# Two transformer blocks on one core: four of the eight norms taken apart, with the rows' roots applied behind the products

## The chip, the core and the metric

One core of a Trainium2 chip runs the whole program: TensorE (PE in the profile, with its weight loads as PEld), VectorE (DVE), ScalarE (ACT), GpSimd (POOL) and SyncE (SP), which issues most of the transfers. The metric is the device time of one execution in microseconds (us), a median over several executions. Lower is better.

## The reference

Input x is 512 tokens of 1024 features. Block one is an attention block (forgetting attention and sparse attention, their outputs gated by two sigmoids) and a mixture of experts. Block two is a feed-forward network (FFN1), a mixer (neighbourhood attention and latent attention) and a second feed-forward network (FFN2). Cut to the norms that the change touches:

```
rms_norm(x, g) = x * rsqrt(mean(x*x) + 1e-6) * g

h = rms_norm(x, norm_mix_g)                        # norm 0, then h @ w_in, 4896 columns
...q, k, v of both attentions; g_a, g_b = last 2048 columns of h @ w_in
x = x + (sigmoid(g_a)*out_a + sigmoid(g_b)*out_b) @ w_out
x = x + moe(rms_norm(x, norm_ffn_g))               # norm 1, stays as it is
f = swiglu(rms_norm(x, ffn1_pre_g), w_gu, w_down)  # norm 2:  (silu(gate) * up) @ w_down
h = x + 0.5 * rms_norm(f, ffn1_post_g)             # a norm behind a stage ("post norm")
z = rms_norm(h, mix_pre_g) @ w_in_2                # norm 3
h = h + rms_norm(mixed, mix_post_g)                # post norm
f = swiglu(rms_norm(h, ffn2_pre_g), ...)           # norm 4
h = h + 0.5 * rms_norm(f, ffn2_post_g)             # post norm, the output
```

## The kernel before

Tokens are four tiles `t` of 128 rows. `xres` (in `xarea`) holds the residual rows, `hn` (in `harea`) the normed rows, `hT_hi` and `hT_lo` (in `tarea`) the features turned, features on the partitions and the 512 tokens along the row. All large products are made three times in fp32r, high by high, high by low, low by high (`products`, L420 to L422): a float is its rounded high part plus what is left. Weights come in units of 128x2048 (1 MB, `feed`, two buffers `raw`); ACT makes the high part of a unit (`split_high`, L405) and DVE the low part (`split_low`, L411). A unit takes 48 products of 128x512 on PE.

At a norm the engines work one after another: ACT squares four tiles and sums them (`norm_squares`, L1486), DVE scales the sum, ACT takes the root, DVE the reciprocal (`row_rstd`), DVE multiplies the rows by the root and the gain (`norm_rows`, L1775), PE turns them in 32 small transposes (`to_features`, L1015), ACT copies the high part out of PSUM (`to_hT`, L1494) and DVE makes the low part (`low_features`, L1803). The first unit's products are taken in parts (`products_in_parts`, L432, L433, L438), so that those that don't need the low features come first. A post norm is `post_squares` (L1501) and `post_norm` (L1790 and L1792: two instructions for each tile). Each engine is a queue in program order; semaphores tie them, and no scheduler moves anything.

Such a turn stands at five places: at the start (norm 0), behind the attentions (norm 1, for the experts), before FFN1 (norm 2), between FFN1 and the mixer (a post norm and norm 3) and between the mixer and FFN2 (a post norm and norm 4). The program ends with a post norm. In an FFN half (`ffn_half`) PE makes gate and up of a chunk `v` (11 chunks a half) in two banks, ACT applies Silu to the gate (L1659), DVE multiplies by up (L2149), ACT and DVE split the result (L1663, L2154), and the down products follow, whose banks 0 to 3 wait for the last chunk (`ff_hid`).

In the first attention phase the products of the two gates (jobs `ga`, `gb`, 16 in all) and of the two up-projections are put into the rounds of the attention as filling (`fill`); ACT takes tanh of a gate straight from PSUM (L1579).

The order in DVE's queue at the start is:

```
norm_rows()
free_gain(4)
split_low(0)
low_features(0)
split_low(1)
dve.wait_ge(s["pos_psum"], 1)
...
split_low(2)
split_low(3)
```

## Time and profile before

| | |
|---|---|
| median of 3 executions | 1990.91 us (1988.08 to 1991.79) |
| profiled execution, its own time | 1985.92 us |
| its span, first to last instruction | 1984.1 us |
| PE busy | 1789.2 us, 90% |
| DVE, ACT, POOL busy | 937.6, 851.4, 246.6 us |
| mean granted TensorE clock | 0.950 |

The page of the profile gives busy times and the costliest groups of instructions. The waits say who stood idle and what ended it; the chain is the sequence of work that ended last, and its rows stand in order of time. A clock of 1.00 is 2.4 GHz and 0.50 is 1.2 GHz.

### The profile page before, as it was taken

The page shows a single profiled execution, that of the slowest core. Times are in us where ns is not written, and L with a number is a line of the kernel's source. Part 1 is how long each engine was busy: PE and PEld are TensorE (multiplying, and loading weights), DVE is VectorE, ACT ScalarE, POOL GpSimd, SP SyncE. Part 2 cuts the span into 40 slices and gives each one's busy share as a digit, 9 for nine tenths or more (in the row PEclk, how much of TensorE's full clock was granted, in tenths as well). Part 3 has the DMA queues.
Part 4 walks back from the last instruction along what each step waited for, and adds up shares of the span by engine and source line. Part 5 has one row for each costly group of instructions (what it writes and reads, how often), then busy time and mean ns, then how long its engine had stood idle before and what let it go on. Part 6 is the DMA issues. An engine that isn't in the chain of part 4 may idle for free.

```text
span 1984.1 us, 22478 instructions
## 1 busy us (share of the span) xinstructions
PE 1789.2 (90%) x8475; PEld 1415.8 (71%) x8475; DVE 937.6 (47%) x1499; ACT 851.4 (43%) x1356; POOL 246.6 (12%) x310
## 2 busy tenths in 40 slices
PE   5996999999769999949999999698788969999996
PEld 4884566667658888838888888586554858888885
DVE  3546333435359999963332232625554353313334
ACT  3224565553338888843222222334566232223222
POOL 2100342220001111200000000511223000000000
PEclk9998999999969999979999999898798989999998
DMA  6223201114459999672323322323000213223321
GB/s 200 85 68 105 65 22 44 46 61 159 181 218 370 386 387 385 243 227 75 106 85 96 106 86 95 91 89 106 12 22 33 64 54 106 90 90 107 105 86 53
DMA packets 161443, 248.39 MB, mean 125 GB/s; under 512 B 11490, under 2 KB 117057, under 8 KB 148416
## 3 DMA queue, kind: packets, MB, share of 16 engines
q1 hardware_dynamic: 152592, 232.30, 34.5%
q0 software_dynamic: 8752, 14.77, 2.4%
q8 instruction: 62, 1.02, 0.2%
q14 instruction: 37, 0.30, 0.0%
HBM read 241.23 MB, written 12.61 MB: 128 GB/s over the span
## 4 chain that ended last, share of the span: by engine, by line
PE 84%; DVE 7%; ACT 3%; issue 3%; DMA 1%; POOL 1%; SPq 0%; DVEq 0%; ACTq 0%; POOLq 0%
PE psum L420 24%; PE psum L422 23%; PE psum L421 23%; PE psum L583 3%; PE psum L603 3%; PE psum L572 2%; PE psum L1015 1%; ACT warea_r L405 1%; PE psum L432 1%; PE psum L1216 1%; DVE harea L1790 1%; DVE xarea L1792 1%; PE psum L433 1%; PE psum L438 1%; DMA const<-in_consts 1%
## 5 line engine op out<-in xcount | busy, mean ns | idle before, releaser
L411 DVE TENSOR_TENSOR warea_r<-warea,warea_r 128x2048 fp32r<-128x2048 f32 x114 | 266.4, 2339 | 394.4 <-ACT warea_r L405 394.3
L405 ACT ACTIVATE warea_r<-warea 128x2048 fp32r<-128x2048 f32 x114 | 217.5, 1910 | 284.3 <-PE psum L422 262.0
L420 PE MATMUL psum<-tarea_r,warea_r 128*128 128x512 f32 x848 | 335.7, 396 | 0.0
L421 PE MATMUL psum<-tarea_r,warea_r 128*128 128x512 f32 x848 | 330.7, 390 | 0.0
L422 PE MATMUL psum<-tarea_r,warea_r 128*128 128x512 f32 x848 | 330.6, 390 | 0.0
L420 PE MATMUL psum<-warea_r,arena_r 128*128 128x512 f32 (+1 forms) x768 | 300.9, 392 | 12.1 <-DVE arena_r L2102 7.3
L422 PE MATMUL psum<-warea_r,arena_r 128*128 128x512 f32 (+1 forms) x768 | 297.3, 387 | 0.0
L421 PE MATMUL psum<-warea_r,arena_r 128*128 128x512 f32 (+1 forms) x768 | 297.2, 387 | 0.0
L420 PEld LDWEIGHTS psum<-tarea_r,warea_r 128*128 128x128 f32 x848 | 159.4, 188 | 37.7 <-issue 5.3
L422 PEld LDWEIGHTS psum<-tarea_r,warea_r 128*128 128x128 f32 x848 | 159.4, 188 | 33.9
L421 PEld LDWEIGHTS psum<-tarea_r,warea_r 128*128 128x128 f32 x848 | 159.6, 188 | 31.6
L1659 ACT ACTIVATE arena<-psum 128x512 f32<-128x512 f32 x44 | 26.3, 599 | 355.4 <-PE psum L422 335.4
L420 PEld LDWEIGHTS psum<-warea_r,arena_r 128*128 128x128 f32 (+1 forms) x768 | 143.7, 187 | 44.0 <-DVE arena_r L2102 7.9
L422 PEld LDWEIGHTS psum<-warea_r,arena_r 128*128 128x128 f32 (+1 forms) x768 | 143.4, 187 | 29.5
L421 PEld LDWEIGHTS psum<-warea_r,arena_r 128*128 128x128 f32 (+1 forms) x768 | 143.6, 187 | 28.0
L2149 DVE TENSOR_TENSOR arena<-psum,arena 128x512 f32<-128x512 f32 x44 | 30.4, 692 | 279.1 <-ACT arena L1659 279.1
L420 PE MATMUL psum<-warea_r,tarea_r 128*128 128x512 f32 (+3 forms) x392 | 149.6, 382 | 1.4 <-DVE tarea_r L2229 1.4
L421 PE MATMUL psum<-warea_r,tarea_r 128*128 128x512 f32 (+3 forms) x392 | 148.7, 379 | 0.0
L422 PE MATMUL psum<-warea_r,tarea_r 128*128 128x512 f32 (+3 forms) x392 | 148.6, 379 | 0.0
L1015 PE MATMUL psum<-const,harea 128*128 128x128 f32 x160 | 27.9, 357 | 85.7 <-DVE harea L1775 85.7
L583 PE MATMUL psum<-arena 64*128 64x256 f32 (+3 forms) x416 | 87.2, 447 | 2.3 <-DVE nmax L642 1.5
L1015 PEld LDWEIGHTS psum<-const,harea 128*128 128x128 f32 x160 | 26.9, 193 | 87.2 <-issue 87.2
(312 smaller groups left out, 2499.2 us busy)
## 6 DMA issues: line engine op xcount, KB each, us to landing
warea<-in_ffn_w_gu SPq DMA_DIRECT2D x88, 512.0 KB, 5.0
warea<-in_w_in SPq DMA_DIRECT2D x48, 512.0 KB, 4.6
warea<-in_ffn_w_down SPq DMA_DIRECT2D x40, 512.0 KB, 4.2
arena<-in_w_up SPq DMA_DIRECT2D x16, 1024.0 KB, 7.3
tarea<-in_w_up SPq DMA_DIRECT2D x16, 1024.0 KB, 7.2
tarea<-in_w_down SPq DMA_DIRECT2D x16, 1024.0 KB, 7.5
warea<-in_w_gate SPq DMA_DIRECT2D x14, 1024.0 KB, 7.8
harea<-in_w_gate SPq DMA_DIRECT2D x14, 1024.0 KB, 7.4
```

What stands on the lines that cost most here:

```text
L405: act.activation(w_hi[:, u % 2, :], raw[:, u % RAW, :], ACT.Copy).then_inc(s["split_hi"], 1)
L411: dve.tensor_tensor(w_lo[:, u % 2, :], raw[:, u % RAW, :], w_hi[:, u % 2, :].bitcast(f32), ALU.subtract)\
L420: nc.tensor.matmul(out, high, by_high, start=first, stop=False)
L421: nc.tensor.matmul(out, high, by_low, start=False, stop=False)
L422: return nc.tensor.matmul(out, low, by_high, start=False, stop=last)
L432: nc.tensor.matmul(out, a_hi, b_hi, start=n == 0, stop=False)
L572: mm = nc.tensor.transpose(bank[0:rows, P * j:P * j + P], pbuf[:, c0:c0 + rows], ident)
L583: mm = nc.tensor.matmul(ps[st["e"]][:, a:b], st["lhsT"], rhs, start=True, stop=not (mask and b == n))
L603: mm = nc.tensor.matmul(half(bank, e_)[:, c:d_], lhsT, PT[0:lhsT.shape[0], e_, j, a:b], start=start, stop=stop)
L1015: mm = nc.tensor.transpose(ps[2 * t + half_][:, P * c:P * c + P], hn[:, t, P * (4 * half_ + c):P * (4 * half_ + c) + P], ident)
L1659: nc.scalar.activation(sgb[:, v % 2, :], ps[2 * (v % 2)], ACT.Silu).then_inc(s["ff_silu"], 1)
L2149: V.tensor_tensor(sgb[:, v % 2, :], ps[2 * (v % 2) + 1], sgb[:, v % 2, :], ALU.mult).then_inc(s["gated"], 1)
```

## The change

Norms 0, 2, 3 and 4 are no longer applied to the rows ahead of the turn.

- PE turns the raw rows as they come (`raw_features`), feature chunk `c` of all tiles into bank `c`.
- The norm's gain is a column per feature chunk (`gain_col`, loaded element by element) and goes in as a scale where ACT makes the high part (`raw_high`) and DVE the low part (`raw_low`), eight instructions each.
- The rows' roots come later (`late_root`): DVE builds a diagonal of them, PE multiplies it by ones (`row_factor`, one product of 128x128 by 128x512), ACT copies the result (`row_copy`), which then holds a root for every token along the row. Results with tokens on the partitions are scaled where they leave PSUM; results with tokens along the row are multiplied by that copy: the 16 gates on DVE ahead of tanh, the gate of each FFN chunk on DVE ahead of Silu (the up half is scaled at the down products' exit), q and k of the mixer on DVE.
- A post norm multiplies the gain into `hn` while the squares are still summed (tile 0 on POOL, tiles 1 to 3 on DVE), and needs one instruction a tile behind the root.
- `products_in_parts` goes; the first unit waits for each feature chunk in turn. In place of eight broadcast loads of gains there are four and four columns. At the start the identity comes ahead of the rows, two weight units ahead of the rest of the constants, and the mask of the neighbourhood attention later.

```diff
@@ SyncE @@
+            sp.dma_start(const[:, 0:P], w["consts"][:, 0:P]).then_inc(s["ident_in"], 16)
             for t in range(NT):
-                sp.dma_start(xres[:, t, :], w["x"][0, t * P:(t + 1) * P, :]).then_inc(s["x_in"], 16)
-            sp.dma_start(const[:, :], w["consts"][:, 0:NCONST]).then_inc(s["const_in"], 16)
-            for u in range(AT_MIX):
+                sp.dma_start(xres[:, t, :], w["x"][0, t * P:(t + 1) * P, :]).then_inc(s[f"rows_in{t}"], 16)
+            for u in range(2):
+                feed(u)
+            sp.dma_start(const[:, P:masks], w["consts"][:, P:masks]).then_inc(s["const_in"], 16)
+            for u in range(2, AT_MIX):
                 feed(u)
@@ GpSimd @@
+            def gain_column(k, name, sem):
+                pool.dma_start(gain_col[k], w[name].rearrange("a (c p) -> p (a c)", p=P)).then_inc(s[sem], 16)
+            def premultiplied(n):
+                pool.wait_ge(s["gain_in"], 16 * (n + 1))
+                pool.wait_ge(s["sumsq"], 4 * (1 + 2 * n) + 1)
+                nc.gpsimd.tensor_tensor(hn[:, 0, :], hn[:, 0, :], gain, ALU.mult).then_inc(s["premul_pool"], 1)
@@ TensorE @@
+            def raw_features(k, ready):
+                for t in range(NT):
+                    ready(t)
+                    for c in range(KD):
+                        mm = nc.tensor.transpose(ps[c][:, P * t:P * t + P], xres[:, t, P * c:P * c + P], ident)
+                        if t == NT - 1:
+                            mm.then_inc(s["ht_psum"], 1)
+            def row_factor(k, bank):
+                pe.wait_ge(s["diag_ready"], LATE.index(k) + 1)
+                nc.tensor.matmul(bank, upper[:, 768:896], row_of[k], start=True, stop=True).then_inc(s["row_psum"], 1)
@@ TensorE, project(n, cols) @@
+                            if n == 0 and t == 0:
+                                pe.wait_ge(s["hT_low_ready"], k + 1)
...
+                    if n == 0 and h:
+                        pe.wait_ge(s["pos_in"], 32)
+                        nc.tensor.transpose(ps[7][:, 0:32], pos_raw, ident[0:32, 0:32]).then_inc(s["pos_psum"], 1)
+                        pe.wait_ge(s["const_in"], 16)
+                        row_factor(0, ps[6])
@@ TensorE, ffn_half(g), gate_up_unit(v) @@
                     for k in range(2):
+                        if g % 2 == 0 and isinstance(v, int) and v == 1 and k:
+                            row_factor((2, 4)[g // 2], ps[7])
@@ ScalarE @@
+            def raw_high(k):
+                act.wait_ge(*((s["cols_late"], 48) if k else (s["col_in0"], 16)))
+                for c in range(KD):
+                    act.wait_ge(s["ht_psum"], 8 * k + c + 1)
+                    nc.scalar.activation(hT_hi[:, c, :], ps[c], ACT.Identity, scale=gain_col[k][:, c:c + 1]).then_inc(s["ht_ready"], 1)
+            def late_features(k):
+                warm()
+                squares(k, range(NT - 1))
+                raw_high(k)
+                squares(k, range(NT - 1, NT))
+                root(late[k])
@@ ScalarE, ffn_half: chunk(v) @@
-                    nc.scalar.activation(sgb[:, v % 2, :], ps[2 * (v % 2)], ACT.Silu).then_inc(s["ff_silu"], 1)
+                    act.wait_ge(s["ff_scaled"], i + (base + v + 1))
+                    nc.scalar.activation(sgb[:, v % 2, :], sgb[:, v % 2, :], ACT.Silu).then_inc(s["ff_silu"], 1)
...
                 for v in range(3):
+                    if v == 0 and g % 2 == 0:
+                        row_copy((2, 4)[g // 2], ps[7])
                     chunk(v)
@@ VectorE @@
+            def late_root(k):
+                norms[0] += 1
+                dve.wait_ge(s["sumsq"], 4 * norms[0])
+                variance(late[k], ss[:, 0:NT], D).then_inc(s["var_ready"], 1)
...
+                V.reciprocal(late[k], late[k]).then_inc(s["late"], 1)
...
+                V.tensor_tensor(row_of[k].rearrange("p (t q) -> p t q", t=NT), view(ident, [[0, NT], [1, P]]),
+                                late[k].unsqueeze(2).to_broadcast([P, NT, P]), ALU.mult).then_inc(s["diag_ready"], 1)
-                    chained(V.scalar_tensor_tensor(out=hn[:, t, :], in0=hn[:, t, :], scalar=rstd[:, t:t + 1],
-                                                   in1=gain[:, k % 2, :], op0=ALU.mult, op1=ALU.mult))
-                    V.scalar_tensor_tensor(out=xres[:, t, :], in0=hn[:, t, :], scalar=factor, in1=xres[:, t, :],
+                    V.scalar_tensor_tensor(out=xres[:, t, :], in0=hn[:, t, :], scalar=rstd[:, t:t + 1], in1=xres[:, t, :],
                                            op0=ALU.mult, op1=ALU.add).then_inc(s["res_ready"], 1)
+            def raw_low(k):
+                for c in range(KD):
+                    dve.wait_ge(s["ht_ready"], 8 * k + c + 1)
+                    V.scalar_tensor_tensor(out=hT_lo[:, c, :], in0=ps[c], scalar=gain_col[k][:, c:c + 1],
+                                           in1=hT_hi[:, c, :].bitcast(f32), op0=ALU.mult, op1=ALU.subtract)\
+                        .then_inc(s["hT_low_ready"], 1)
-            norm_rows()
-            free_gain(4)
             split_low(0)
-            low_features(0)
+            raw_low(0)
             split_low(1)
+            late_root(0)
             dve.wait_ge(s["pos_psum"], 1)
@@ VectorE, ffn_half: chunk(v) @@
+                    unit_through(dve, u0 + v, i)
+                    V.tensor_tensor(sgb[:, v % 2, :], ps[2 * (v % 2)], row_of[(2, 4)[g // 2]], ALU.mult).then_inc(s["ff_scaled"], 1)
                     dve.wait_ge(s["ff_silu"], i + (base + v + 1))
@@ VectorE, first attention phase, ahead of a round's scores @@
+            def gate_rows(m):
...
+                        V.tensor_tensor((tan_a if kind == "ga" else tan_b)[j], ps[fill_bank(job)], row_of[0], ALU.mult)\
+                            .then_inc(s["gate_scaled"], 1)
```

How the rows stand now at three places. First the head of DVE's queue, of before (the `warea_r` rows are `split_low`, L1803 is `low_features`, L1812 to L1814 copy the turned positions out of bank 7):

```order
L1755 TENSOR_SCALAR rstd<-ss 128x4
L1761 RECIPROCAL rstd<-rstd 128x4
L1775 SCALAR_TENSOR_TENSOR harea<-xarea,rstd,garea 128x1024 x4
L1782 MEMSET nmax 128x1
L411 TENSOR_TENSOR warea_r<-warea,warea_r 128x2048
L1803 TENSOR_TENSOR tarea_r<-psum,tarea_r 128x4x128 x8
L411 TENSOR_TENSOR warea_r<-warea,warea_r 128x2048
L1812 COPY small<-psum 128x32
L1813 COPY small<-psum 64x32
```

and the same place of the change (L416 is `split_low`, L1870 `raw_low`, L1797 to L1837 `late_root`, L1879 to L1881 the copies of the positions):

```order
L416 TENSOR_TENSOR warea_r<-warea,warea_r 128x2048
L1870 SCALAR_TENSOR_TENSOR tarea_r<-psum,small,tarea_r 128x512 x8
L416 TENSOR_TENSOR warea_r<-warea,warea_r 128x2048
L1797 TENSOR_SCALAR small<-ss 128x4
L1833 RECIPROCAL small<-small 128x4
L1837 TENSOR_TENSOR const<-const,small 128x512
L1879 COPY small<-psum 128x32
L1880 COPY small<-psum 64x32
L1881 COPY small<-psum 64x32
L416 TENSOR_TENSOR warea_r<-warea,warea_r 128x2048 x2
L1920 TENSOR_SCALAR small<-small 64x1
```

The norm's rows have gone from the head, and the root stands behind the second unit's split. The copies stand ahead of the splits of units 2 and 3 as they did, but what they wait for stands in PE's queue behind unit 1 now instead of behind unit 0.

Second, DVE between the last down products of FFN1 and the mixer's first products, of the change (L2252 takes the down products out, L1844 multiplies the gain in, L1860 adds to the residual):

```order
L2252 SCALAR_TENSOR_TENSOR harea<-psum,small,harea 128x512 x8
L1844 TENSOR_TENSOR harea<-harea,garea 128x1024 x2
L1854 TENSOR_SCALAR rstd<-ss 128x4
L1844 TENSOR_TENSOR harea<-harea,garea 128x1024
L1803 RECIPROCAL rstd<-rstd 128x4
L1860 SCALAR_TENSOR_TENSOR xarea<-harea,rstd,xarea 128x1024 x4
L1864 MEMSET nmax 128x1
L416 TENSOR_TENSOR warea_r<-warea,warea_r 128x2048
L1870 SCALAR_TENSOR_TENSOR tarea_r<-psum,small,tarea_r 128x512 x8
L416 TENSOR_TENSOR warea_r<-warea,warea_r 128x2048
```

Before, one split stood ahead of the post norm, eight instructions of 128x1024 made the post norm, and four more the norm behind it. Now the split stands behind the residual, and seven instructions of 128x1024 are left.

Third, ACT at the head of FFN1, of the change (L1497 squares, L1518 `raw_high`, L1523 `row_copy`, L1701 Silu, L410 `split_high`, L1705 the high part of a chunk):

```order
L1497 ACTIVATE harea,ss<-xarea 128x1024 x3
L1518 ACTIVATE tarea_r<-psum,small 128x512 x8
L1497 ACTIVATE harea,ss<-xarea 128x1024
L1478 ACTIVATE small<-small 128x4
L1523 ACTIVATE garea<-psum 128x512
L1701 ACT_TABLE_LOAD
L1701 ACTIVATE arena<-arena 128x512
L410 ACTIVATE warea_r<-warea 128x2048
L1705 ACTIVATE arena_r<-arena 128x512
```

The copy of the rows' factors stands ahead of the table load, of the first Silu and of the split of unit 2; before, the table load came right behind the features.

## Rows read from the trace of the kernel before

**Rows 1.** Page, part 1: busy us, share of the span, instructions.

```profile
PE 1789.2 (90%) x8475; PEld 1415.8 (71%) x8475; DVE 937.6 (47%) x1499; ACT 851.4 (43%) x1356; POOL 246.6 (12%) x310
```

**Rows 2.** Waits of PE, whole span: us in total, times, longest.

```profile
PE psum L1015 <- DVE harea L1775: 85.7, 5, 25.6
```

**Rows 3.** Chain between FFN1 and the mixer: start us, us, what.

```profile
1250.27 5.45 DVE harea L2171 x8
1255.72 2.20 DVE warea_r L411
...
1258.49 1.30 DVE harea L1790
1259.81 1.22 DVE xarea L1792
...
1271.70 5.47 PE psum L1015 x32
...
1278.06 0.47 PE psum L432
```

**Rows 4.** Instructions of lines 2283 and 1122: ns min/median/max, first and last start.

```profile
L2283 DVE SCALAR_TENSOR_TENSOR harea<-psum,rstd,harea x8: 743/746/751, 1568.6 to 1586.1; 128x512 f32<-128x512 f32 x8
...
L1122 PE MATMUL psum<-arena,const x6: 1052/1135/1217, 196.0 to 202.6; 8*128 8x512 f32 x6
```

**Rows 5.** Timeline of POOL and of DVE in the projections.

```profile
52.64 3.60 POOL L918 TENSOR_TENSOR harea<-arena 128x2048 f32<-128x2048 f32 x1 [38.15 <-ACT arena L1516]
...
54.40 4.00 DVE L411 TENSOR_TENSOR warea_r<-warea,warea_r 128x2048 fp32r<-128x2048 f32 x1 [9.35 <-ACT warea_r L405]
```

**Rows 6.** Timeline between the mixer and FFN2, by engine.

```profile
1588.07 0.17 DVE L1755 TENSOR_SCALAR rstd<-ss 128x4 f32<-128x4 f32 x1 [1.22 <-ACT arena L1501]
...
1608.66 0.47 PE L432 MATMUL psum<-tarea_r,warea_r 128*128 128x512 f32 x1 [0.84 <-issue]
```

**Rows 7.** Timeline before FFN1, by engine.

```profile
879.85 5.12 DVE L2136 SCALAR_TENSOR_TENSOR xarea<-tarea,arena,xarea 128x1024 f32<-128x1024 f32 x4
...
895.05 1.28 ACT L1659 ACT_TABLE_LOAD   x1
...
895.13 0.47 PE L432 MATMUL psum<-tarea_r,warea_r 128*128 128x512 f32 x1 [0.84 <-issue]
```

**Rows 8.** Windows of PE before FFN1: us, busy (instructions), granted clock, DMA share, GB/s.

```profile
865.00:866.00 1.00, 0.00 (x0) 0.88 0.12 37
...
888.00:889.00 1.00, 0.73 (x4) 0.50 0.33 85
...
893.00:894.00 1.00, 1.00 (x10) 0.96 0.51 193
```

**Rows 9.** Timeline at the start: start us, us, instruction, idle before it.

```profile
22.36 1.91 ACT L405 ACTIVATE warea_r<-warea 128x2048 fp32r<-128x2048 f32 x1 [1.07 <-DMA warea<-in_w_in]
...
29.48 0.47 PE L432 MATMUL psum<-warea_r,tarea_r 128*128 128x512 f32 x1 [1.31 <-DVE tarea_r L1803]
...
40.85 0.19 DVE L1812 COPY small<-psum 128x32 f32<-128x32 f32 x1 [5.13 <-PE psum L1038]
```

**Rows 10.** Timeline of DVE and PE at a half's last chunk.

```profile
1019.77 0.68 DVE L2154 TENSOR_TENSOR arena_r<-arena,arena_r 128x512 f32 x1
...
1020.51 0.50 PE L420 MATMUL psum<-warea_r,arena_r 128*128 128x512 f32 x1
```

**Rows 11.** DMA view, 0 to 60 us in 40 slices; an issue: KB, us to landing.

```profile
GB/s 0 183 371 391 344 134 238 328 385 392 330 276 156 234 388 336 20 0 0 16 254 403 26 0 53 355 302 0 0 0 40 281 376 3 0 0 0 0 0 63
...
small<-in_na_out_norm_g POOLq DMA_DIRECT2D x1, 2.0 KB, 8.2
```

**Rows 12.** Chain at the end of the program.

```profile
1963.81 5.46 DVE harea L2171 x8
...
1979.82 1.23 DVE xarea L1792
```

**Rows 13.** Windows in the first attention phase: us, busy of PE, PEld, DVE, ACT, POOL.

```profile
260.00:320.00 60.00, 59.31 (x346) 40.67 (x344) 21.74 (x95) 34.94 (x102) 20.30 (x31) 1.00 0.11 36
```

More of the change, by code:

```diff
@@ L982, in _ @@
             scatter(x_now)
-            for k in range(2, 5):
-                load_gain(k)
+            load_gain(1)
+            premultiplied(1)
             pool.wait_ge(s["fd_psum"], 16)
@@ new lines, in premultiply, with post_norm @@
+            def premultiply(t):
+                dve.wait_ge(s["gain_in"], 16 * (gains_used[0] + 1))
+                dve.wait_ge(s["sumsq"], 4 * norms[0] + t + 1)
+                V.tensor_tensor(hn[:, t, :], hn[:, t, :], gain, ALU.mult).then_inc(s["premul"], 1)
+            def post_norm(factor, done=()):
+                for t in range(1, NT - 1):
+                    if t not in done:
+                        premultiply(t)
+                dve.wait_ge(s["sumsq"], 4 * norms[0] + 4)
+                f2 = factor ** -2
+                V.tensor_scalar(rstd[:, 0:NT], ss[:, 0:NT], f2 / D, f2 * 1e-6, ALU.mult, ALU.add).then_inc(s["var_ready"], 1)
+                premultiply(NT - 1)
+                inverse_root(rstd[:, 0:NT])
+                n = gains_used[0]
```

277 lines of the change are left out of this document (142 added, 135 removed).

## The prediction

> **What bounds the kernel now.** The page's busy line says that PE works 90% of the span [rows 1], so time can come only out of PE's idle tenth or out of PE's own work. Who makes PE wait is read next: the five transposes at the turns waited 85.7 us for the normed rows, 25.6 us at most [rows 2]. Four of these five turns are what the change rewrites. Then the chain across the turn between FFN1 and the mixer shows what the wait is made of: DVE takes out the last down products until 1255.72, splits a unit (2.20), works eight instructions of 1.21 to 1.30 on the post norm, four more on the norm, PE turns for 5.47, and the first product starts at 1278.06 [rows 3]. Nothing in it runs beside anything else; PE has no product for 22.3 us. So the price of a turn is the time from its last input to the first product, and I work it out anew for each from rows. Then I look for what waits in its place.
>
> **Mixer turn (post norm and norm 3).** Counted from 1255.72. Now: two gain multiplications of 128x1024, half of a 2.20 us split each [rows 3], 2.2; a third behind the variance, 1.1, and the reciprocal and variance, 0.4; four adds of 1.22, 4.9; the split that had stood in front, 2.2; the first low part, 0.75 as the nearest form, a scaled subtraction out of PSUM [rows 4]. PE's turning and ACT's high part lie beside the split. POOL's multiplication of tile 0 is 1.8 (half of 3.60 [rows 5]) and can start when ACT has squared tile 0, some 1.5 ahead of DVE's last output by my estimate, so it may hold DVE for 0.3. Sum 11.9: first product at 1267.6 instead of 1278.06. Gain 10.4. The row factor costs PE one fp32 product of 512 columns, 1.05 [rows 4]: 9.4 left. The features then come every 0.7, which is what PE needs for three products: eight results of three products each left PE in 5.45 [rows 3], 0.68 a result and 0.227 a product. So no later loss.
>
> The port is where a page can be weighed. DVE's split took 4.00 beside POOL's multiplication, against 2.20 alone [rows 3, 5]: it stood still until POOL was done at 56.24. The Trainium skill, SBUF — State Buffer, section SBUF: two separate sides, says that a DVE instruction with two SBUF inputs and a GpSimd one shut each other out for the whole instruction; the trace agrees. By that rule the instructions that read PSUM are spared, and the 0.3 stays 0.3; were all of DVE held, the turn would lose 1.8.
>
> **FFN2 turn (post norm and norm 4).** The variance stands at 1588.07 [rows 6]. Two multiplications are done by then. 0.2 for it, 1.1 for the third, 0.2 for the reciprocal, 4.9 for the adds: rows done at 1594.5. A transpose (0.3), the high part (0.7, taken like the low part), the low part 0.75 and their signals 0.2: first product at 1596.5 instead of 1608.66 [rows 6]. Gain 12.2, less 1.05.
>
> **FFN1 turn (norm 2).** The rows are done at 879.85 + 5.12 = 885.0 [rows 7]; first product at 885.0 + 2.0 = 887.0 instead of 895.13. Gain 8.1, less 1.05. Here the clock counts: it had left 1.00 by 866, and it came back only at about 893, five after PE had begun to turn at about 888.3 [rows 8]. Before, the slow stretch lay on the transposes; now they are spread over the rows' arrival and the products themselves may start slow. Bounds: none, if the spread transposes raise it, and 2.5 (five us at half speed). I take 1.5. At the other two turns the transposes follow each other every 1.2, at half speed about as long as that, and bring the clock back in time: nothing.
>
> **A new wait in both FFNs.** ACT's queue now has row copy, table load, Silu, split of unit 2 in a row (third order piece). The row factor comes behind three groups of 24 products, 16.3 after the first product, and ends at +17.4. Then 0.6 copy, 1.28 table load [rows 7], 0.6 Silu, 1.91 split high [rows 9], 2.3 split low, 0.7 low part of chunk 0: +24.8. PE has finished unit 1 at +22.8 and needs both for unit 2. Stall 2.0, twice: 4.0. Bounds 0 and 2 x 3.
>
> **The halves' ends.** The last chunk's low part ended at 1019.77 + 0.68 = 1020.45 and the bank's next product began at 1020.51 [rows 10]: that chain is just in time. The change puts a multiplication of 0.69 and a signal ahead of Silu. So 0.75 is late in each of four halves: 3.0. Elsewhere in the loop the same 0.75 is covered by 5 us of slack.
>
> **The start (norm 0).** Now the first product stands at 29.48, and the first unit's split, on ACT since 22.36, had waited for its data [rows 9]. The transfers moved, summed over the slices of 1.5 us, about 6.2 MB until then [rows 11]. With constants and gain behind it, unit 0 has 3.2 MB ahead of or in it, and the slices reach that near 12.5 us. The slice from 7.5 runs at 134 and those from 16.5 to 21 at 276, 156 and 234, where transfers of single elements are under way; a column of 512 elements took 8.2 to land [rows 11], the new ones have 1024. That costs perhaps 2 more. Unit 0 at 14.5, high 1.9, low 2.3, first low features 0.75: product at 19.5. Gain 10, bounds 6 (unit 0 at 18.5) and 12. Now against it: PE turns early, then stands idle for over 5 us; as before FFN1 the clock may have fallen when the products start, 2.0 (0 to 2.5). And DVE's copies of the positions wait for PE behind unit 1 and stand ahead of the split of unit 2 (first order pieces; the copy waits for PE [rows 9]): copies 0.6, split 2.3, signals 0.2 from the end of unit 1, during which PE only has the row factor: 3.1, of which 0.2 was there before. Left: 10 - 2.0 - 2.9 = 5.1.
>
> The Trainium skill, DMA: Bandwidth & Descriptors, section Rules for kernel authors, speaks against the columns: a strided last dimension becomes one descriptor for each element. The trace shows the slow slices but not what such a column delays. By the page the first column's 1024 elements could keep unit 0 back to the bound above, and the gain would be 1.1.
>
> **The end.** Down products out at 1969.27; two multiplications 2.2, variance 0.2, the third 1.1, reciprocal 0.2, adds 4.9: 1977.9 instead of 1979.82 + 1.23 = 1981.05 [rows 12]. The four stores now follow each other every 1.2, faster than 0.5 MB at the 390 GB/s of [rows 11] (1.35): 0.3 back. Gain 2.8.
>
> **Gates in the first attention phase.** 16 multiplications of 0.7 go onto DVE, which is busy 21.7 of 60 us there while PE is busy 59.3 [rows 13]. PE hides them; if one is on its path it costs 0.75 (12 in all). I take 1.0. Table loads, the two more ACT squares behind the features, the q and k copies now on DVE and the mask's later load have whole units of 10.9 as cover: nothing; without it a table load would be 1.28.
>
> **Sum.** Mixer 9.4, FFN2 12.2 - 1.05 - 2.0 = 9.1, FFN1 8.1 - 1.05 - 1.5 - 2.0 = 3.6, start 5.1, end 2.8: 30.0. Less the halves 3.0 and the gates 1.0: **26.0 us**. The profiled execution, 1985.9, goes to 1959.9. The median shown is 5.0 higher, 1990.9, so 1964.9; I say 1965.
>
> **Rivals.**
> - *More than that.* The chains have slack that I don't see: no stall at unit 2 (+4), halves hidden (+3), clocks in time (+3.5), gates free (+1). For it: slack was measured at one half only. Against it: every instruction of the stall chain has a row. 37.5 us, 1953.
> - *The start gives nothing back.* The columns or the order of the queues hold unit 0 or the gain until the old time less 2, so that 8 of the 10 are lost; the clock is slow at the two later turns too, 1.5 each. For it: small elements slow the transfers [rows 11]. Against it: unit 0 has half of the old bytes ahead of it. 26 - 11 = 15, 1976.
> - *Slower.* The gate's bank is freed by DVE and no longer by ACT, and DVE carries the splits of 2.2 and stands in order. If the multiplication lies behind a split, PE waits 2.2 + 0.75 for the bank. All 16 so: 47 us, and 1990.9 - 27 + 47 = 2011; it decides from 10 of the 16. Against it: by the code ten splits are spread over the 64 rounds of this phase, and DVE is idle two thirds of it [rows 13].
>
> **How the numbers follow.** The forecast has 0.68 (1957 to 1972 by the bounds of start, clock and stalls), more gain 0.12, the start 0.14, slower 0.03; 0.03 is for several losses that end near nothing. The range 1952 to 1977 takes the first three in all but their tails. A measurement of this kernel can tell 0.2% (4 us) from no change. Faster 0.95, same 0.02, slower 0.03.
>
> **What would show it.** First products near 19.5, and 8, 12 and 10 us closer behind the last input at the three later turns. A PE wait of 2 us ahead of unit 2 in FFN1 and FFN2, one of 3 us ahead of unit 2 of the projections, 0.7 at bank 0 in four halves. The clock at 0.50 in the first products of the start and FFN1. The first attention phase as long as before. The prediction is wrong if raw features come slower than every 0.7, so that PE paces on ACT and DVE for a whole unit, or if PE's waits at the gates grow.

## The result: 12 us faster, not 26

The changed kernel takes 1979.13 us (median of 5, 1974.25 to 1979.71), the kernel before in the same set 1990.91 (median of 5): the ratio is 0.9948, 95% interval 0.9936 to 0.996. That is 11.8 us; forecast were 26, and 1979 lies above the range. Once more in a later set it was 0.994 (0.9926 to 0.9953). Of the six executions of the first experiment below, one of 2645 us at a granted clock of 0.64 is not counted. The profiled executions differ by less, 1984.1 to 1977.9 in their spans, since the one of before happens to be 5 us under its median. The ledger below is of these two spans, so its sum is 6.2.

The page of the changed kernel, busy time of the engines; [rows 1] has before's PE at 1789.2:

```profile
PE 1811.5 (92%) x8483; PEld 1428.6 (72%) x8483; DVE 966.3 (49%) x1548; ACT 858.6 (43%) x1355; POOL 254.5 (13%) x313
```

PE is busy 22 us more with almost the same instructions. The four row factors are 1.1 each, 4 to 5 of the 22; a good part of the rest is that products follow each other every 0.227 at full clock and every 0.43 at half, and slow products count as busy time. Its waits (us in total, times, longest), against the 85.7 of [rows 2]:

```profile
PE psum L1020 <- DVE xarea L2214: 16.6, 4, 15.0
PE psum L1020 <- DVE xarea L1860: 11.5, 2, 6.6
PE psum L425 <- DVE tarea_r L1870: 11.1, 4, 9.2
...
PE psum L425 <- DVE warea_r L416: 7.5, 3, 5.4
...
PE psum L425 <- DVE arena_r L2235: 6.9, 6, 2.0
```

The transposes (L1020) now wait for raw rows, 28 us. New are 9.2 ahead of the very first product (L1870, low features), 5.4 for the split of a unit (L416) and the six waits for a chunk's low part (L2235): four of 0.74 for the last chunk of a half, and two of 2.0 for chunk 0, ahead of unit 2 of each FFN.

The span cut at the same instructions in both traces (us by which the changed kernel is shorter; "again" is its second profile, from a later set):

| stretch | forecast | measured | again |
|---|---|---|---|
| start, to the turning of the first heads | +5.1 | -3.8 | -4.3 |
| first attention phase, to the first residual | -1.0 | -4.6 | -4.6 |
| experts and FFN1 turn, to FFN1's first product | +8.1 | +7.9 | +7.6 |
| FFN1, to the last down product | -6.0 | -7.3 | -7.2 |
| mixer turn | +10.4 | +10.0 | +10.0 |
| mixer | -1.0 | -3.0 | -2.7 |
| FFN2 turn | +12.2 | +10.4 | +10.4 |
| FFN2 | -4.6 | -6.3 | -6.3 |
| end | +2.8 | +2.9 | +2.9 |

The turns came as forecast, 31.2 of 33.5. What failed is at the start (8.9) and in the four stretches behind the start and the turns (8.6 together).

**Start.** The timeline of the changed kernel, one row for each engine's part (start, duration, in brackets the idle time before it and what ended it); it answers to [rows 9]:

```profile
16.78 1.91 ACT L410 ACTIVATE warea_r<-warea 128x2048 fp32r<-128x2048 f32 x1 [14.79 <-DMA warea<-in_w_in]
...
46.70 0.19 DVE L1879 COPY small<-psum 128x32 f32<-128x32 f32 x1 [14.54 <-PE psum L1065]
...
47.33 7.92 DVE L416 TENSOR_TENSOR warea_r<-warea,warea_r 128x2048 fp32r<-128x2048 f32 x2
...
47.30 3.59 POOL L923 TENSOR_TENSOR harea<-arena 128x2048 f32<-128x2048 f32 x1 [29.67 <-ACT arena L1557]
...
53.10 0.79 PE L425 MATMUL psum<-warea_r,tarea_r 128*128 128x512 f32 x1 [5.38 <-DVE warea_r L416]
```

Unit 0 landed at 16.76 and the first product stood at 21.82. DVE took the positions at 46.70 and then needed 7.92 for two splits of 2.3: POOL's squares of the first four tiles of z, the result of the projection, had begun at 47.30, 0.03 earlier, and DVE stood until they were done at 50.9. PE waited 5.38 and came back at half clock (windows of 5 us: PE busy, PE's instructions that touch the window, granted clock, DMA share, GB/s):

```profile
45.00:50.00 5.00, 2.72 (x10) 1.00 0.00 0
50.00:55.00 5.00, 1.90 (x5) 0.63 0.16 23
55.00:60.00 5.00, 5.00 (x17) 0.68 1.03 380
```

**FFN1, at the stall of unit 2.** The same view, ahead of the stall, right behind it, and the next 5 us:

```profile
918.00:922.00 4.00, 2.03 (x9) 0.97 0.00 0
922.00:927.00 5.00, 5.00 (x17) 0.69 0.76 210
927.00:932.00 5.00, 5.00 (x24) 1.00 0.77 209
```

The stall is the forecast 2.0, but 17 products follow in 5 us in place of 24: 7 x 0.227 = 1.6 more.

**FFN2 turn**, PE: the mixer's last product ends at 1587.0, then the transposes and the first product, 12.2 behind it (before, 22.6):

```profile
1591.84 6.47 PE L1020 MATMUL psum<-const,xarea 128*128 128x128 f32 x32 [4.88 <-DVE xarea L1860]
1599.12 0.47 PE L425 MATMUL psum<-tarea_r,warea_r 128*128 128x512 f32 x1 [0.81 <-DVE tarea_r L1870]
```

Of the 32 transposes, 27 follow each other every 0.21, 1.7 for a tile of eight, and only the last five every 0.11. That is slower than the rows come (1.2), so the transposes end 3.0 behind the last row. At the FFN1 turn, where PE waits for each tile, all run at the slow pace and a tile takes 1.97 from its first start to its last end.

### The profile page after: what moved, and what is told of

Same layout as the page of the kernel before. It is cut to its first block, busy times and chain, and to the rows that moved or that the text cites. A ratio compares the mean times of both kernels' runs of the same rounds, so it can differ in the third digit from the quotient of the medians.

```text
span 1977.9 us, 22533 instructions
## 1 busy us (share of the span) xinstructions
PE 1811.5 (92%) x8483; PEld 1428.6 (72%) x8483; DVE 966.3 (49%) x1548; ACT 858.6 (43%) x1355; POOL 254.5 (13%) x313
## 4 chain that ended last, share of the span: by engine, by line
PE 83%; DVE 6%; ACT 4%; issue 3%; DMA 1%; POOL 1%; SPq 0%; DVEq 0%; ACTq 0%; POOLq 0%
PE psum L425 24%; PE psum L426 23%; PE psum L427 23%; PE psum L570 3%; PE psum L590 3%; PE psum L559 2%; ACT warea_r L410 2%; DVE warea_r L416 1%; PE psum L1232 1%; DMA warea<-in_w_in 1%; POOL arena L690 1%; PE psum L1138 1%; PE psum L1020 1%; DVE xarea L2214 1%; PE psum L1401 0%
## 5 line engine op out<-in xcount | busy, mean ns | idle before, releaser
L416 DVE TENSOR_TENSOR warea_r<-warea,warea_r 128x2048 fp32r<-128x2048 f32 x114 | 268.0, 2353 | 388.7 <-ACT warea_r L410 388.5
L425 PE MATMUL psum<-tarea_r,warea_r 128*128 128x512 f32 x896 | 358.2, 400 | 5.9 <-DVE arena_r L2235 3.9
L426 PE MATMUL psum<-tarea_r,warea_r 128*128 128x512 f32 x896 | 351.7, 393 | 0.0
L427 PE MATMUL psum<-tarea_r,warea_r 128*128 128x512 f32 x896 | 351.4, 392 | 0.0
L410 ACT ACTIVATE warea_r<-warea 128x2048 fp32r<-128x2048 f32 x114 | 217.2, 1907 | 303.2 <-PE psum L427 288.4
L425 PEld LDWEIGHTS psum<-tarea_r,warea_r 128*128 128x128 f32 x896 | 169.5, 189 | 48.3 <-issue 7.7
L427 PEld LDWEIGHTS psum<-tarea_r,warea_r 128*128 128x128 f32 x896 | 169.9, 190 | 36.3
L426 PEld LDWEIGHTS psum<-tarea_r,warea_r 128*128 128x128 f32 x896 | 169.8, 190 | 34.1 <-issue 0.7
L425 PE MATMUL psum<-warea_r,tarea_r 128*128 128x512 f32 (+3 forms) x408 | 158.9, 390 | 15.9 <-DVE tarea_r L1870 9.2
L1701 ACT ACTIVATE arena<-arena 128x512 f32<-128x512 f32 x44 | 27.8, 632 | 328.9 <-DVE arena L2228 328.8
L426 PE MATMUL psum<-warea_r,tarea_r 128*128 128x512 f32 (+3 forms) x408 | 157.4, 386 | 0.0
L427 PE MATMUL psum<-warea_r,tarea_r 128*128 128x512 f32 (+3 forms) x408 | 157.2, 385 | 0.0
L2228 DVE TENSOR_TENSOR arena<-psum,garea 128x512 f32<-128x512 f32 x44 | 30.4, 691 | 221.1 <-PE psum L427 197.5
L892 POOL TENSOR_TENSOR harea<-harea,garea 128x1024 f32<-128x1024 f32 x3 | 7.2, 2389 | 807.5 <-ACT arena L1538 807.5
L425 PEld LDWEIGHTS psum<-warea_r,tarea_r 128*128 128x128 f32 x408 | 79.3, 194 | 30.9 <-DVE warea_r L416 15.6
```

Of the source, the lines that this page charges most:

```text
L410: act.activation(w_hi[:, u % 2, :], raw[:, u % RAW, :], ACT.Copy).then_inc(s["split_hi"], 1)
L416: dve.tensor_tensor(w_lo[:, u % 2, :], raw[:, u % RAW, :], w_hi[:, u % 2, :].bitcast(f32), ALU.subtract)\
L425: nc.tensor.matmul(out, high, by_high, start=first, stop=False)
L426: nc.tensor.matmul(out, high, by_low, start=False, stop=False)
L427: return nc.tensor.matmul(out, low, by_high, start=False, stop=last)
L1701: nc.scalar.activation(sgb[:, v % 2, :], sgb[:, v % 2, :], ACT.Silu).then_inc(s["ff_silu"], 1)
```

## The experiments

All are the changed kernel with one edit unless said. "Less" and "more" are against the changed kernel, by the ratio to the kernel before (0.9948; a thousandth is 2.0 us); stretches are those of the table. The changed kernel itself gave 0.9948 and 0.994, and its intervals overlap those of several experiments, so 2 or 3 us of a whole time are not told from nothing by it. What an edit did is read from the stretch that it touches.

### Which part of the start's stall is order, which POOL's port

```
             split_low(1)
             late_root(0)
+            split_low(2)
             dve.wait_ge(s["pos_psum"], 1)
...
-            split_low(2)
             split_low(3)
```

> One edit to the changed kernel: DVE makes the low part of unit 2 before it waits for the turned positions, no longer behind the three copies. Theory A (order, then the port): PE waited 5.4 us ahead of unit 2 because the split stood behind the wait for the positions and then behind POOL's squares; with the split done by about 40 PE runs on behind the row factor at 47.7 and its clock stays at 1.00, which also gives back 12 products at half speed (2.5). Sum 7.9 off the changed kernel: about 1971. Theory B (my prediction's size of it): the order costs 2.9 and no clock: about 1976. Theory C (POOL's squares, wherever the split stands, hold DVE and the next split takes the wait over): the heads' transposes stay near 77.5 and the time near 1979.

Measured: 1974.03 us, ratio 0.9922 (0.991 to 0.9935), 5 us less. The stall is gone, and so is the slow stretch behind it; the heads come 8.0 earlier, the 7.9 of theory A. The same windows:

```profile
45.00:50.00 5.00, 5.00 (x21) 1.00 0.00 0
50.00:55.00 5.00, 5.00 (x24) 1.00 0.15 21
```

The first attention phase of this execution was 3.1 longer than in the changed kernel's, so the span shows 3.2 of the 8.0. The whole time, 1974, lies between theories A and B; what decides is the start, where the 8.0 speak against B (2.9) and C (nothing).

```
+                if g == 0:
+                    pool.wait_ge(s["split_lo"], 3)
                 if g < 3:
                     nc.gpsimd.tensor_tensor(sq, zs[g], zs[g], ALU.mult).then_inc(s["sq_done"], 1)
```

> The order on DVE stays as in the changed kernel; POOL begins its squares of the first four z tiles only when the low part of unit 2 is there. It parts the stall of 6.7 us (end of unit 1 to unit 2) into order and port. Theory A: the split then takes 2.3 instead of 5.6, PE starts unit 2 near 49.7 instead of 53.1, a stall of 2.0 behind the row factor as I had predicted, and whether the clock stays at 1.00 after a pause that short shows in the first products of unit 2: 3.4 to 5.9 us less than the changed kernel, 1973 to 1976. Theory C (POOL is not what holds the split): unit 2 still starts near 53, no change, 1979.

Measured: 1974.27, ratio 0.9933 (0.9914 to 0.9952), 3 us less. DVE's two splits in their old place, and PE's first product of unit 2:

```profile
45.34 4.49 DVE L416 TENSOR_TENSOR warea_r<-warea,warea_r 128x2048 fp32r<-128x2048 f32 x2
...
47.69 0.50 PE L425 MATMUL psum<-warea_r,tarea_r 128*128 128x512 f32 x1 [1.95 <-DVE warea_r L416]
```

4.49 in place of 7.92, a wait of 1.95 in place of 5.38. So of 5.4 the order cost 2.0, which I had forecast, and the port 3.4, which I had not. The expectation also asked whether the clock stays up behind so short a pause. It did not: in the 5 us from 47.7 it was 0.66, and 15 products ran, 7 fewer than at the full pace of 0.227 (1.6 us). Here DVE is the one that starts first: its second split began at 47.55, POOL's squares at 47.79, and they took 5.50 in place of 3.59.

### What held unit 0 back

```
             gain_column(0, "norm_mix_g", "col_in0")
+            pool.wait_ge(raw_in[0], 16 * len(units[0]))
             for k, name in enumerate(("fox_q_g", ...
```

> The changed kernel, with POOL's small loads (all but the first gain column) issued only when unit 0 has landed. Unit 0 landed at 16.76, 2.3 later than the bytes ahead of it would make it. If small elements on the queues are what delays it, it lands near 14.5 and the first product stands near 19.5 instead of 21.8, with the whole about 2 us shorter. Rival: what delays it is the queue's own pace at the start (identity, rows and two units, 3.2 MB at the rates of the slices), and it lands within 0.5 us of 16.76.

Measured: 1974.39 (one execution). ACT's split of unit 0 and the first product:

```profile
12.54 1.91 ACT L410 ACTIVATE warea_r<-warea 128x2048 fp32r<-128x2048 f32 x1 [10.53 <-DMA warea<-in_w_in]
...
17.58 0.77 PE L425 MATMUL psum<-warea_r,tarea_r 128*128 128x512 f32 x1 [6.63 <-DVE tarea_r L1871]
```

Unit 0 landed 4.2 earlier, at 12.5, not 2.3. One execution would be thin, but every profile says the same: with the small loads behind it unit 0 landed between 12.2 and 13.6 (six kernels), with them in front between 15.5 and 19.7 (eleven), and the first product then fell between 20.5 and 24.8: 4 us of spread from here alone. The first column's 1024 elements stand ahead in all of them and do no harm that shows. The three later columns can be no more than a part of it. In the changed kernel POOL issued the first of them here:

```profile
11.64 0.99 POOL L885 DMA_DIRECT2D small<-in_ffn_pre_g  x1
```

By then the fourth tile of rows had already landed 1.7 later than in this run, at 11.53 in place of 9.81. How the delay is shared out among the small loads is not shown. Before the change most of them stood in front as well.

### The start with all mends, and its clock

```
-            split_high(0)
-            raw_high(0)
+            raw_high(0, range(4))
+            split_high(0)
+            raw_high(0, range(4, KD))
             split_high(1)
```

DVE's low parts are ordered in the same way; the two edits above are in it (first and third).

> The start of the changed kernel, mended in three places: unit 2's low part ahead of the copies, the small loads behind unit 0, and the first four feature tiles taken ahead of unit 0's split (which needs only these). First product at 16.8 (17.6 with the small loads late alone, less the four low parts that no longer stand behind the split). The clock: PE stands idle from the last transpose to 16.8, so I still expect 0.50 at the first products, 2.5 us lost. Gain on the changed kernel 5.0 + 8.0 = 13, less what a fuller first attention phase takes (the first of these edits alone lost 3 of its 8.5 again by the experts): 10 +- 3, 1969. Rival: the gains are given back in the attention phase until the old time less 5, 1974.

Measured: 1971.8, ratio 0.9915 (0.99 to 0.9931), 6.6 less; the heads 12.3 earlier. That is no more than the two edits above gave alone (8.0, and 4.2 for unit 0). The new one gave nothing: unit 0 landed at 12.19, and the first product came 5.8 later in place of 5.1, at 17.97 and not at 16.8, because ACT was still at the features, with a table load ahead of them:

```profile
10.07 1.28 ACT L1519 ACT_TABLE_LOAD   x1 [10.07 <-PE psum L1021]
...
13.67 1.92 ACT L410 ACTIVATE warea_r<-warea 128x2048 fp32r<-128x2048 f32 x1
```

Part of the gain was lost behind it: the first attention phase was 2.5 longer than in the changed kernel. The next kernel adds, behind the raw transposes:

```
+            pe.wait_ge(s["hT_low_ready"], 1)
+            for c in range(16):
+                nc.tensor.transpose(ps[0][:, P * (c % 4):P * (c % 4) + P], ident, ident)
```

> The same start, and PE turns the identity 16 times into bank 0 as soon as that bank is free, in the time in which it would stand idle before the first product. It parts the clock from the rest of the start. If the slow first products come from that idle time, the granted clock is 1.00 (or is back within two products) from the first product on, and the end of unit 0's products comes 2.0 to 2.5 earlier than in the kernel without the turnings, with the first product in the same place. Rival: a clock that rises only after some time of real products, the same 12 at half speed; then no change but for the turnings' own 0.3 if they run late.

Measured: 1969.84, ratio 0.9911 (0.9894 to 0.9927). The first product came 0.67 later in its profile, yet the heads came 1.5 earlier: 2.15 by the clock, as expected. The windows of the kernel without the turnings, then with them:

```profile
20.00:25.00 5.00, 5.00 (x18) 0.73 0.97 266
```

```profile
20.00:25.00 5.00, 5.00 (x24) 1.00 0.93 234
```

### The stall at unit 2 in FFN1 and FFN2

```
                 for v in range(3):
-                    if v == 0 and g % 2 == 0:
+                    if first_of_two(v):
+                        split_high(u0 + 2)
                         row_copy((2, 4)[g // 2], ps[7])
...
+                    if first_chunk:
+                        split_low(u0 + 2)
                         dve.wait_ge(s["row_ready"], (2, 4)[g // 2])
```

The first part is ACT's, the second DVE's; both splits are taken out of chunk 0, where they stood.

> The changed kernel, with the split of unit 2 of FFN1 and FFN2 put ahead of the row copy on ACT and ahead of the wait for the row factor on DVE. In the changed kernel PE waits 2.0 us ahead of unit 2 for the low part of chunk 0, twice. By my order argument the chain behind the row factor gets shorter by the split (1.9 on ACT), and PE's wait goes from 2.0 to nothing or 0.3 in each FFN: about 3.8 us less, 1975. Rival: the table load or the row factor's own place (it ends 17.4 behind the first product) holds chunk 0, and the wait stays over 1.5: 1978 to 1979.

Measured: 1971.32, ratio 0.9912 (0.9897 to 0.9927): 7 us less, where 3.8 were expected. Both stalls are gone, and with them the slow products behind them; from FFN1's first product to the mixer's it is 4.0 shorter (0.9 of that a faster start, below), FFN2 3.8. The waits of PE in FFN1:

```profile
PE psum L425 <- DVE arena_r L2243: 1.5, 2, 0.7
PE psum L425 <- DVE tarea_r L1875: 0.5, 1, 0.5
```

The first line is FFN1's share, two of the four waits of 0.74 at the halves.

### The halves

```
-                    for m in (4, 5, 6, 7, 0, 1, 2, 3) if j == 0 else range(8):
+                    for m in (4, 5, 6, 7, 2, 3, 0, 1) if j == 0 else range(8):
```

> The changed kernel, with the first down unit of each half beginning in banks 4, 5, 6, 7, 2, 3 and only then 0 and 1, the two that the last chunk frees. That gives the last chunk 2.7 us more. PE's four waits of 0.74 for the last chunk's low part go away: 3.0 us less than the changed kernel, 1976. Rival: the wait only moves to another bank or to the next unit (its split stands behind the last chunk on DVE too): no change, 1979.

Measured: 1976.03, ratio 0.9937 (0.9923 to 0.9951), 2 us less. The waits of 0.74 are not there any more, in either FFN; FFN1's and FFN2's waits for the chunk's low part are the one of 2.0 each. So 3.0 was the right price, 0.74 four times. In this profile the clock stayed up behind FFN1's stall, which is luck and not the edit.

### PE's clock at the later turns

```
                 for t in range(NT):
+                    for c in range(0 if not k else 20 if t == 0 else 6 if k == 2 else 0):
+                        nc.tensor.transpose(ps[c % KD][:, P * (NT - 1):P * NT], ident, ident)
                     ready(t)
```

> The changed kernel, and PE turns the identity 20 times ahead of the raw rows at the three later turns (and 6 times between the row tiles at FFN1), into places that the real turnings write again. In the changed kernel PE stood idle for 5 us or more ahead of these turns and its transposes then took 0.246 each, 1.97 a tile of rows, where the rows come every 1.2. If that idle time is what sets the clock, they take 0.16, 1.3 a tile: the first product comes 1.5 sooner behind the last down product at FFN2, 0.5 to 1 at the mixer, 0.7 at FFN1 with none of the first products slow (0.9): 3.5 to 4 us less, 1975. Rival: the rows' adds on DVE, 1.2 each, are the pace and the clock is hidden behind them: under 1 us, 1978.

Measured: 1973.45, ratio 0.9926 (0.9911 to 0.9941), 4.4 less. PE at the FFN2 turn:

```profile
1584.12 2.40 PE L1019 MATMUL psum<-const 128*128 128x128 f32 x20 [0.85 <-DVE harea L2382]
1588.04 4.68 PE L1022 MATMUL psum<-const,xarea 128*128 128x128 f32 x32 [1.53 <-DVE xarea L1862]
1593.68 0.47 PE L425 MATMUL psum<-tarea_r,warea_r 128*128 128x512 f32 x1 [0.95 <-DVE tarea_r L1872]
```

The transposes take 4.68 in place of 6.47, which is the rows' pace; the FFN2 turn gains 12.2, the forecast's number: 1.7 less in the turn, 1.5 less from the mixer's first product to FFN2's. FFN1's first products ran fast (22 in 5 us, not 18; 0.9). At the mixer turn nothing came, since PE was idle again between the turnings and the rows. The third part I had not expected: the stalls of 2.0 at unit 2 are still there, and in this execution the clock stayed at 1.00 behind both (22 products started in 5 us, not 15), 1.6 and 1.5.

### The gates

Left out (the rows' roots on both sets of gates are not computed here; ACT takes the tanh from the bank):

```
-                        V.tensor_tensor(..., ps[fill_bank(job)], row_of[0], ALU.mult).then_inc(s["gate_scaled"], 1)
...
-                        nc.scalar.activation(t_, t_, ACT.Tanh, scale=0.5)
+                        nc.scalar.activation(t_, ps[fill_bank(job)], ACT.Tanh, scale=0.5)
```

> The changed kernel without the 16 multiplications of the gates by the rows' roots: ACT takes the tanh straight from the bank, as before the change, and the bank is free when ACT has it. Left out of the computation: the rows' roots on the two sets of gates. My prediction had 1.0 us for them: then 1978. The traces say that the first attention phase became 4.2 longer, 2.5 of it in waits of PE: if the multiplications on DVE are the cause, 1975, with the phase from the first forget product to the residual back at its old length. If only the rest of that 4.2 is left (a phase that falls differently because all is shifted), 1979.

Measured: 1976.03, ratio 0.9937 (0.9925 to 0.9949), 2 us less, though unit 0 landed 3 late in its profile. The first attention phase is 0.9 longer than before the change, not 4.6. PE's waits in it:

```profile
PE psum L559 <- POOL xarea L692: 3.6, 3, 1.2
...
PE psum L559 <- ACT harea L663: 0.6, 1, 0.6
```

and in the changed kernel:

```profile
PE psum L559 <- POOL xarea L692: 4.7, 3, 1.7
...
PE psum L559 <- ACT harea L663: 1.4, 1, 1.4
```

1.9 more in four waits. Much of the other half is the clock: in the 10 us behind the third wait of L692 it is 1.00 in the kernel without the multiplications (wait 1.19) and 0.83 in the changed one (wait 1.74).

The two halves are not equally well known. PE's idle time in this phase repeats: 27.0 us before the change and in this run, 28.9 in each of the eleven profiled kernels that have the multiplications at a round's opening and no other edit there. What PE takes besides does not: 414.7 before, 415.7 here, and 417.2 to 420.6 in those eleven. So 1.9 is the sure part of the price, and the rest, 1.5 to 4.9, depends on the clock of the execution.

Multiplication and tanh at the end of a round:

```
             def fill(m):
+                gate_rows(m)             # DVE; no longer at the round's opening
...
             def split(m):
+                fill(m)                  # ACT: the tanh behind the exp
```

> The changed kernel, with the gates' multiplications at the end of a DVE round (behind its scores) in place of its opening, and their tanh at the end of ACT's round. Without the multiplications the first attention phase was 3.8 us shorter (from the forget product to the first residual). If it is their place, 0.7 ahead of the scores for which exp, POOL and PE wait in turn, most of the 3.8 comes back: 1976. If the price is DVE's work itself or the bank that now comes free later, the phase stays as long as in the changed kernel or gets longer by waits of PE for the bank: 1979 or more.

Measured: 1996.97, ratio 1.0043 (1.0027 to 1.0058), 19 us more. The phase is 23.7 longer than before the change, 19.0 longer than in the changed kernel:

```profile
PE psum L425 <- DVE garea L2034: 7.1, 4, 1.8
```

PE waits for the gate's bank, which the multiplication (L2034) frees. This is the mechanism of my "slower" rival, brought about. The waits are 7 of the 19; for the other 12 PE is busy but slower, with a mean granted clock of 0.93 in the phase in place of 0.95.

The tanh alone moved (the second of these edits):

> The changed kernel, with the gates' multiplications where they are (opening of a DVE round), but ACT's tanh at the end of its round in place of the start. The traces show ACT waiting for the multiplication (0.69) and only then going on to the tanh, the exp and the split of a unit, which DVE waits for in turn. If this series is the price of the gates, the first attention phase comes back to the length that it had without the multiplications, 3.5 to 4 us less: 1975 to 1976. If the 0.69 on DVE ahead of the scores is the price, it stays as long as in the changed kernel, within 1 us.

Measured: 1977.59, ratio 0.9946 (0.9932 to 0.9959), no change; the phase 3.9 longer than before the change. My theory of the series on ACT fell. Then DVE's work itself doubled:

```
+                        V.tensor_reduce(small[:, 558:559], ps[fill_bank(job)], AX.X, ALU.add)
                         V.tensor_tensor((tan_a if kind == "ga" else tan_b)[j], ps[fill_bank(job)], row_of[0], ALU.mult)
```

> The changed kernel, and DVE reads each gate's bank a second time (a sum over its 512 columns into one unused column) ahead of the multiplication: the time that DVE works on a gate about doubles, from 0.7 to 1.3 or 1.4, in the same place. If the price of the gates is that DVE work ahead of the scores, the first attention phase gets longer by about as much again as the multiplications made it, 3 to 4 us (res1 behind the forget product: 8 to 9 longer than in the kernel before), and the whole is 1981 to 1983. If it is only the signal and the order behind it, or a fixed wait for the bank, the phase stays within 1 us of the changed kernel's.

Measured: 1984.41, ratio 0.9977 (0.9961 to 0.9992), 6 us more. The phase is 10.1 longer than before: 0.9 without, 4.6 with, 10.1 with twice the work. PE's idle time in it goes 27.0, 28.9, 30.2, and none of it is a wait for the gate's bank; PE waits ahead of the scores' products (L559), for POOL and ACT. So a price of DVE's time ahead of the scores is shown, 1.3 to 1.9 us of waits for 0.7 on each of the 16 gates. The remaining 4.1 of the last step is PE at a lower clock, of which up to 3.1 also came in kernels with no edit here, so its size is not shown.

### The changed kernel again, and everything together

> The changed kernel itself, once more, on the chip of these runs. For the yardstick: 0.994 to 0.996 of the kernel before. For the spread of its start and of its clock: the first product between 20.8 and 24.8 (as in the kernels with the same start), 17 or 18 products in the five microseconds behind each FFN's stall at unit 2 where the clock falls, 24 where it doesn't.

Measured: 1977.22, ratio 0.994 (0.9926 to 0.9953); the stretches are in the table above, 18 products in the first 5 us of FFN1 (22 at the full pace), 15 behind each stall.

> All edits so far together, without the one on the gates' place: unit 2's low part first, small loads behind unit 0, four feature tiles ahead of unit 0's split, the identity turned in the idle time at the start and at the turns, the split of unit 2 first in the FFNs, and the banks' order. By the traces of each alone: start 13.8 (heads' transposes at 63.6 in place of 77.3), FFNs 4.8 and 3.8, banks 1.5 each, turns 3.5; sum 28.9 on the changed kernel, 1950. Bounds: the attention phases differed by up to 3 us from one run to another, and if the turns give nothing it is 1954. Rival: an earlier start meets units that have not landed yet, or the halves' splits become late: over 1958.

Measured: 1951.43, ratio 0.9812 (0.9799 to 0.9825): by the ratio 27 us less than the changed kernel, where 28.9 were expected, and 37 less than before. Start 13.8, FFN1 with the mixer turn 6.9, mixer with FFN2 turn 1.5, FFN2 5.9 by the stretches. The windows in which the changed kernel had 10 and 5 products:

```profile
45.00:50.00 5.00, 5.00 (x24) 1.00 0.32 92
50.00:55.00 5.00, 5.00 (x24) 1.00 0.32 121
```

With the gates at the end of a round too:

> The same, with the gates' multiplications and tanh at the end of a round as well. If their place is what costs, 3 to 4 us less than the kernel with all the others: 1947. If not, the same 1950.

Measured: 1970.93, ratio 0.9921 (0.9906 to 0.9935), the same loss of some 20. With the tanh alone moved:

> The kernel with all edits (1951.4) with ACT's tanh at the end of the round as well. 3.5 to 4 us less if the tanh behind the multiplication is the price: 1947 to 1948. Otherwise the same.

Measured: 1951.19, ratio 0.9814 (0.9799 to 0.9829), no change.

## Where the prediction was right and where not

Of the 19.8 us between the forecast and the two spans, the start makes 8.9, the first attention phase 3.6, the FFNs 3.0, the turns 2.3 and the mixer 2.0.

- **Turns: right.** 10.0 of 10.4, 7.9 of 8.1, 10.4 of 12.2, the end 2.9 of 2.8. At FFN2 the failed step is the sentence that the transposes at half speed take "about as long as that" (1.2 a tile). Back to back they take 1.7; turning the identity ahead of them gave 1.7 back, and with it the turn gained the 12.2.
- **Start: wrong, by 8.9.** Three steps: the landing of unit 0 (2.3), the stall ahead of unit 2 (3.5) and the clock (2.4 behind the stall, 0.5 at the first products). "Perhaps 2 more" for transfers of single elements: it was 4.2. I weighed the first column; the loads behind it on POOL's queue did the harm. The Trainium skill, DMA: Bandwidth & Descriptors, Rules for kernel authors, speaks against strided columns, which become one descriptor for each element. The trace does not show them to be the cause: with the first one still ahead unit 0 landed at 12.5, and 1.7 of the 4.2 was there before POOL issued the first of the other three. "Copies 0.6, split 2.3, signals 0.2": the order was right and cost 2.0, but POOL's squares begin as DVE does, 3.4 more. I had the pair of [rows 5] before me, used it at the mixer turn and did not ask where POOL would stand at the start; by the Trainium skill, SBUF — State Buffer, SBUF: two separate sides, the one that starts first keeps the other out, and the trace agrees: 47.30 against 47.33. And the clock was charged for the first products (2.0, measured 2.15 to 2.5) but not for those behind the stall, 2.4 again; a stall of 2.0 would have cost 1.6 of it too.
- **Stalls at unit 2: 2.0 right, twice.** Missing was the clock behind them: 1.6 each. With it and the first products of FFN1 (0.9 for 1.5) the FFNs come to -7.3 and -6.3.
- **Halves: right**, 0.74 four times.
- **Gates: 1.0 forecast, 3.7 measured in one pair of profiles**, 1.9 of it in waits of PE. The failed step is "PE hides them". "DVE is idle two thirds" is true and decided nothing: the multiplication stands at a round's opening, ahead of the scores for which exp, POOL and PE wait. My bound, 12 for all 16 on the path, held it. By my own sign, "if PE's waits at the gates grow", this part was wrong.
- **Mixer: 1.9 more than the row factor.** Between the mixer's first product and its last, executions of kernels that do not differ there lay between 0.2 under and 3.5 over the kernel before. PE's idle time there is no longer than before (33.5 us against 34.2), so the 1.9 is PE at a slower pace, as in the attention phase. What sets it is not shown.
- **Rivals.** Nearest came "the start gives nothing back", 1976, by another way: unit 0 and the stall together took more than all of the start's gain. "More" and "slower" did not come; the latter's mechanism is real (the run with the gates later) but the change leaves the multiplication at the opening, where the bank comes free in time.

## What to carry to other kernels

A new wait is to be priced with the clock behind it: at unit 2 of both FFNs the stall's length was right and its aftermath, 1.6 each, was left out, and at the start the aftermath was 2.4. When an instruction moves, look at what the other engines do in that very microsecond, port and queue, not at their share of busy time. And when a stage is nearly bound by PE, idle time that cannot be removed can be filled with turnings of the identity, and a factor that is needed late should stand behind the work that PE needs soon: with the other edits these were worth more (27 us) than the change itself (12).

## What the runs showed of the hardware

A pause of PE as short as 2.0 us mostly took the clock down. Behind the 26 stalls of 2.0 at unit 2, in 13 profiled kernels that have them, 15 products started in the next 5 us in 21 cases (granted clock 0.66 in the changed kernel), and 22, the full pace, in the other 5. The kernel before has three waits of 1.19 in the first attention phase: in the 10 us behind the first the clock was 0.83, behind the other two 1.00, and the same in the kernel without the multiplications. Which pauses escape is open; both stalls did in the kernel with the turnings. A phase with the same instructions and the same idle time of PE (28.9 us) took between 446.1 and 449.5 us, so the clock alone spreads a stretch by 3 us from one execution to another. And small loads counted for more than their bytes: 0.46 MB on POOL's queue held back unit 0, which SP's queue loads, by 4.2 us, where that many bytes at the 390 GB/s of [rows 11] would take 1.2 (an estimate). Whether the small pieces or the queue do it, the runs do not tell.
